# FFN input of a two-block transformer kernel: the activations' high and low parts as one 512-column operand, and new places in SBUF

## The reference

```
h = h + rms_norm(swiglu_ffn(rms_norm(h, norm_ffn_pre[l]), w_ffn_in[l], w_ffn_out[l]), norm_ffn_post[l])
# swiglu_ffn(u, w_in, w_out): z = u @ w_in (1024 x 5632), split in halves of 2816 columns each;
#                             (silu(one half) * (the other half)) @ w_out (2816 x 1024)
```

## Time and profile before

| | |
|---|---|
| median of three runs | 1117.15 us |
| the profiled execution | 1118.65 us |
| its span, first to last instruction | 1117.3 us |
| mean granted TensorE clock | 0.992 |
| FFN input f0, f1 (PE, with the waits in them) | 626.2 to 751.2 us, 924.8 to 1049.8 us |
| FFN output g0, g1 | from 751.2 us, from 1049.8 us |

### The profile page before, as it was taken

The page is one execution under the profiler, slowest core; times in us unless marked ns, Lnnn a source line. Parts: engine busy times, 40 slices in busy tenths (PEclk is TensorE's granted clock), DMA queues, the critical chain, the costliest instruction groups (busy, mean ns, idle before and its releaser), DMA issues.

```text
span 1117.3 us, 19183 instructions
## 1 busy us (share of the span) xinstructions
PE 1091.6 (98%) x7736; PEld 995.6 (89%) x7736; DVE 759.7 (68%) x1416; ACT 592.2 (53%) x1050; POOL 47.2 (4%) x48
## 2 busy tenths in 40 slices
PE   8999999899899999999999999999999999999998
PEld 7998888889699999789987899997889779999986
DVE  3588786997678887776677666674466466666643
ACT  4475583555576666335355744454474367444542
POOL 0260000010000000110000000000000000000000
PEclk9999998999999999999999999999999999999999
DMA  9965942554345554664442475545544134555441
GB/s 361 384 215 223 375 190 78 218 195 152 113 171 189 189 189 170 267 241 158 165 151 91 163 272 189 189 170 174 189 165 156 71 135 162 199 184 184 162 164 38
DMA packets 30764, 208.14 MB, mean 186 GB/s; under 512 B 3538, under 2 KB 4050, under 8 KB 6996
## 3 DMA queue, kind: packets, MB, share of 16 engines
q1 hardware_dynamic: 30676, 206.91, 51.4%
HBM read 205.85 MB, written 1.05 MB: 185 GB/s over the span
## 4 chain that ended last, share of the span: by engine, by line
PE 84%; DVE 11%; ACT 3%; issue 2%; DVEq 0%; ACTq 0%
PE ps L409 45%; PE ps L1730 19%; PE ps L643 3%; DVE wlo L368 3%; PE ps L1508 2%; PE ps L427 2%; DVE tm L582 2%; PE ps L2396 1%; PE ps L2428 1%; PE ps L836 1%; PE ps L1857 1%; ACT whi L360 1%; PE ps L652 1%; PE ps L1362 1%; PE ps L440 1%
## 5 line engine op out<-in xcount | busy, mean ns | idle before, releaser
L368 DVE TENSOR_TENSOR wlo<-raw,whi 128x1024 fp32r<-128x1024 f32 (+2 forms) x328 | 372.7, 1178 | 210.5 <-ACT whi L360 210.1
L360 ACT ACTIVATE whi<-raw 128x1024 fp32r<-128x1024 f32 (+2 forms) x328 | 315.7, 1011 | 156.6 <-PE ps L1730 100.8
L409 PE MATMUL ps<-H_h,whi 128*128 128x256 f32 x1376 | 390.5, 284 | 0.0
L409 PE MATMUL ps<-H_h,wlo 128*128 128x256 f32 x1376 | 385.1, 280 | 0.0
L409 PE MATMUL ps<-H_l,whi 128*128 128x256 f32 x1376 | 384.9, 280 | 0.0
L409 PEld LDWEIGHTS ps<-H_h,whi 128*128 128x128 f32 x1376 | 259.4, 189 | 1.9 <-issue 1.7
L409 PEld LDWEIGHTS ps<-H_l,whi 128*128 128x128 f32 x1376 | 259.6, 189 | 0.7 <-issue 0.5
L409 PEld LDWEIGHTS ps<-H_h,wlo 128*128 128x128 f32 x1376 | 259.9, 189 | 0.0
L1730 PE MATMUL ps<-whi,gl_h 128*128 128x512 f32 x264 | 105.3, 399 | 0.6 <-DVE wlo L368 0.6
L1730 PE MATMUL ps<-whi,gl_l 128*128 128x512 f32 x264 | 104.2, 395 | 0.0
L1730 PE MATMUL ps<-wlo,gl_h 128*128 128x512 f32 x264 | 103.8, 393 | 0.0
(11 more groups left out here) (465 smaller groups left out, 1686.7 us busy)
## 6 DMA issues: line engine op xcount, KB each, us to landing
raw<-f SPq DMA_DIRECT2D x44, 1024.0 KB, 4.8
raw<-win SPq DMA_DIRECT2D x27, 1024.0 KB, 6.8
raw<-ada SPq DMA_DIRECT2D x24, 1024.0 KB, 5.1
raw<-up SPq DMA_DIRECT2D x22, 1024.0 KB, 4.8
raw<-g SPq DMA_DIRECT2D x20, 1024.0 KB, 4.8
raw<-pw SPq DMA_DIRECT2D x12, 1024.0 KB, 4.8
raw<-down SPq DMA_DIRECT2D x10, 1024.0 KB, 5.4
raw<-wa SPq DMA_DIRECT2D x4, 1024.0 KB, 10.2
```

The lines of the kernel that those rows point to most:

```text
L360: act.activation(whi[j % NS][:, a:b], raw_of(key)[:, a:b], ACT.Copy).then_inc(w_hi.hit(key, half), 1)
L368: dve.tensor_tensor(wlo[j % NS][:, a:b], raw_of(key)[:, a:b], whi[j % NS][:, a:b].bitcast(F32), ALU.subtract).then_inc(w_lo.hit(key, half), 1)
L409: ins_ = pe.matmul(bank[:, m * 256:(m + 1) * 256], wt[a][:, kt * w + col + m * 128:kt * w + col + m * 128 + 128], act[b][:, k0 + kt, :], s ...
```

## The change

In the two FFN inputs, high and low part of the activations stand side by side in one tensor (`HF`: per k 256 columns high, then 256 columns low). For each m and k PE now issues two matmuls (`double_pe`): the high weights by all 512 columns into a whole bank, and the low weights by the 256 high columns into its left half. So a unit takes two banks (one for each m), and three pairs of banks take turns; 1/rms gets bank 2. The left half of a bank holds two of the three products, the right half the third, so they have to be added: ACT copies both right halves to `uw` (`low_act`), DVE adds the left halves (`total`), and `scale` multiplies `uw` in SBUF.

The order on ACT and DVE changes with it: ACT does `low_act` behind `next_hi`, then `late_hi`, then SiLU; DVE does `total` behind `next_lo`, then `mul_dve`, then `scale`.

In SBUF, `whi`, `wlo`, `HF`, `gl` and `yc` now all have the remainder 384 by 512 bytes. All other users of `H` get it as a view of the same memory that begins 96 bytes later (remainder 480); its high and low tiles alternate. The rest lies at multiples of 32 bytes.

```diff
-        at = -(-(place[0] - lead[0]) // 128) * 128 + lead[0] if n >= 1024 else place[0]
+        at = place[0] if step == 32 else -(-(place[0] - 384) // step) * step + 384
...
-            lead[0] = 32 * (len(whi) + len(wlo))
-            to.append(sb(f"{name}{i}", [128, 2048], F32R))
-    H = pair("H", 8)
+            to.append(sb(f"{name}{i}", [128, 2048], F32R, 512))
+    Hs = sb("H", [128, 8 * 512 + 32], F32R, 512)
+
+    def halves_of(a):
+        hl = Hs[:, a:a + 4096].rearrange("p (k t) -> p k t", t=512)
+        return hl[:, :, 0:256], hl[:, :, 256:512], hl
+
+    HF = halves_of(0)
+    H = halves_of(24)[0:2]
...
-    gl = pair("gl", NF)
+    gl = pair("gl", NF, 512)
...
+    BANK_PAIRS = (0, 3, 5)
+
+    def double_pe(pe, n, c, ready, hook):
+
+        key, first = (n, c), BANK_PAIRS[c % 3]
+        for i in (first, first + 1):
+            ring, at = (G, i) if i < 3 else (M, i - 3)
+            if ring.free[at]:
+                pe.wait_ge(*ring.free[at])
+            ring.free[at] = u_sum(n, c)
+        where[key] = psum[:, first:first + 2, :]
+        j = SAT[key]
+        hi, lo = whi[j % NS], wlo[j % NS]
+        asked = set()
+        for m, kt in [(m, kt) for kt in range(8) for m in range(2)] if c == 0 else [(m, kt) for m in range(2) for kt in range(8)]:
+            if kt // 4 not in asked:
+                asked.add(kt // 4)
+                pe.wait_ge(*w_lo(key, kt // 4))
+            if c == 0 and m == 0:
+                pe.wait_ge(*ready(kt))
+                hook(kt)
+            a = kt * 256 + m * 128
+            for part in ("lo", "hi") if kt else ("hi", "lo"):
+                if part == "hi":
+                    ins_ = pe.matmul(banks[first + m], hi[:, a:a + 128], HF[2][:, kt, :], start=kt == 0, stop=kt == 7)
+                else:
+                    pe.matmul(banks[first + m][:, 0:256], lo[:, a:a + 128], HF[0][:, kt, :], start=False, stop=False,
+                              skip_group_check=True)
+        ins_.then_inc(unit.hit(*key), 1)
+
     def ffn_pe(pe, n, gen, hook):
         for c in range(NF):
-            gemm_pe(pe, (n, c), H, normed(gen) if c == 0 else held, u_rn(n, c), by_k=c == 0, hook=hook if c == 0 else None)
+            double_pe(pe, n, c, normed(gen), hook)
             if c == 1:
-                rn_pe(pe, gen)
+                rn_pe(pe, gen, True)
+
+    def low_act(act, n, c):
+        act.wait_ge(*unit(n, c))
+        if c >= 3:
+            act.wait_ge(*u_mul(n, c - 3))
+        act.activation(uw[c % 3][:], where[n, c][:, :, 256:512], ACT.Copy).then_inc(u_low.hit(n, c), 1)
...
     def ffn_dve(dve, n, gen):
+        def total(c):
+            dve.wait_ge(*unit(n, c))
+            dve.wait_ge(*u_low(n, c))
+            dve.tensor_tensor(uw[c % 3][:], where[n, c][:, :, 0:256], uw[c % 3][:], ALU.add).then_inc(u_sum.hit(n, c), 1)
+
         def scale(c):
             if c == 0:
                 dve.wait_ge(*rn_set(gen))
-            dve.wait_ge(*unit(n, c))
-            dve.tensor_tensor(uw[c % 3][:], v2(where[n, c][:]), bc2(rn[:]), ALU.mult).then_inc(u_rn.hit(n, c), 1)
+            dve.wait_ge(*u_sum(n, c))
+            dve.tensor_tensor(uw[c % 3][:], uw[c % 3][:], bc2(rn[:]), ALU.mult).then_inc(u_rn.hit(n, c), 1)
```

More of the change, by code:

```diff
@@ L154, in build, with sb @@
 def build(nc, ins, out):
-    place, lead = [-(-nc.sbuf_base // 64) * 64], [0]
-    def sb(name, shape, dt=F32):
+    place = [-(-nc.sbuf_base // 64) * 64]
+    def sb(name, shape, dt=F32, step=32):
         n = 4
@@ L161, in sb, with pair @@
             n *= k
-        at = -(-(place[0] - lead[0]) // 128) * 128 + lead[0] if n >= 1024 else place[0]
+        at = place[0] if step == 32 else -(-(place[0] - 384) // step) * step + 384
         place[0] = at + -(-n // 32) * 32
         return nc.alloc_sbuf_tensor_at(name, shape, dt, offset=at)
-    def pair(name, nch):
-        return sb(name + "_h", [128, nch, 256], F32R), sb(name + "_l", [128, nch, 256], F32R)
+    def pair(name, nch, step=32):
+        return sb(name + "_h", [128, nch, 256], F32R, step), sb(name + "_l", [128, nch, 256], F32R, step)
     par, con = sb("par_sb", [128, NPAR]), sb("con_sb", [128, NCON])
-    sst, epst = sb("sst", [128, 72]), sb("epst", [128, 8])
-    cs, ce = sb("cs", [128, 8]), sb("ce", [128, 8])
     mod, gmod = sb("mod", [128, 48]), sb("gmod", [128, 16])
@@ L251, in build @@
     mh = [sb(f"mh{i}", [128, 384]) for i in range(3)]
-    yc = pair("yc", 8)
+    yc = pair("yc", 8, 512)
     place[0] = block2
@@ L265, in build @@
     tap_f = nc.alloc_sbuf_tensor_at("tap_f", [95, 384], F32R, offset=dft_at + 4 * 768)
-    banks = [nc.alloc_psum_tensor(f"ps{i}", [128, 512], F32) for i in range(8)]
+    psum = nc.alloc_psum_tensor("ps", [128, 8, 512], F32)
+    banks = [psum[:, i, :] for i in range(8)]
     SB, TB, OB = banks[3:5], banks[5:7], banks[7]
@@ L1888, in xtile, with spread_act @@
         return where["xt", gen, k % 4][:, k // 4 * 256:k // 4 * 256 + 256]
-    def spread_act(act, gen, gain):
+    def spread_act(act, gen, gain, to=H):
         for k in range(8):
@@ L1894, in spread_act, with spread_dve @@
                 act.wait_ge(*n_lo(gen, k - 4))
-            act.activation(H[0][:, k, :], xtile(gen, k), ACT.Copy, scale=gain(k)).then_inc(n_hi.hit(gen, k), 1)
-    def spread_dve(dve, gen, gain):
+            act.activation(to[0][:, k, :], xtile(gen, k), ACT.Copy, scale=gain(k)).then_inc(n_hi.hit(gen, k), 1)
+    def spread_dve(dve, gen, gain, to=H):
         for k in range(8):
             dve.wait_ge(*n_hi(gen, k))
-            dve.scalar_tensor_tensor(out=H[1][:, k, :], in0=xtile(gen, k), scalar=gain(k), in1=H[0][:, k, :].bitcast(F32),
+            dve.scalar_tensor_tensor(out=to[1][:, k, :], in0=xtile(gen, k), scalar=gain(k), in1=to[0][:, k, :].bitcast(F32),
                                      op0=ALU.mult, op1=ALU.subtract).then_inc(n_lo.hit(gen, k), 1)
@@ L1908, in xroots_act, with rn_pe @@
             root_act(act, gen, t)
-    def rn_pe(pe, gen):
-        b, old = M.take(rn_set(gen))
+    def rn_pe(pe, gen, apart=False):
+        if apart:
+            b, old, G.free[2] = banks[2], G.free[2], rn_set(gen)
+        else:
+            b, old = M.take(rn_set(gen))
         if old:
@@ L2071, in ffn_dve @@
             if c > 0:
-                scale(c - 1)
+                total(c - 1)
             if c > 1:
                 mul_dve(dve, n, c - 2)
+            if c > 0:
+                scale(c - 1)
             if c > 2:
@@ L2078, in ffn_dve @@
                 tap_parts_dve(dve, (c - 18) // 2)
+        total(NF - 1)
+        mul_dve(dve, n, NF - 2)
         scale(NF - 1)
-        mul_dve(dve, n, NF - 2)
         late_lo(dve, n, NF - 3)
```

19 lines of the change are left out of this document (13 added, 6 removed).

## The result

The changed kernel took 1120.43 us (median of seven runs, 1120.16 to 1122.18), the kernel before beside it 1117.04 us (seven runs, 1113.49 to 1117.26). The ratio is 1.0043, 95% interval 1.0030 to 1.0055: slower by 3.4 us by the medians and by 4.8 us by the ratio, where 1.5 us less had been forecast. The profiled execution took 1122.18 us, with a span of 1120.9 us against 1117.3.

The account below looks back on a forecast made before the run. It took PE's matmul steps as the bound (PE busy 98%, chain 84% on PE). Terms -3.9 - 1.3 + 0.8 + 2.9 = -1.5 us gave a median of 1115.6 us, range 1106 to 1121.5.

Parts of the forecast that it names:

- Step of PE elsewhere: PE outside the FFN input: wide matmuls with `gl` stationary -1.3 us, 64 units with `H` moving +0.8 us.
- equal places collide: Rival: operand reads at the same place hinder each other in each matmul, slow steps become the rule; +7 us, chance 0.08.
- Wide steps in g: 792 wide matmuls of g0, g1 and first `down`: step 0.230 for 0.2317 us, -1.3 us, bounds -2.9 and +2.6.
- The FFN input: PE in f0 and f1: a unit takes 5.554 us against 5.642, -3.9 us over 44 units.
- The circle: Loop of ACT and DVE per FFN-input unit: 5.36 us, fits into 5.554 with 0.19 to spare, cost zero.
- Start of the FFN: First units of the FFN input: `whi` starts 0.65 us later, unit 3 still ready 0.6 us early, no cost.
- The ends: End of each FFN input, ACT and DVE chain: 1.47 us later, twice, +2.9 us, bounds 2.4 and 3.4.
- the circle that does not fit: Rival: in f0 and f1 the ACT and DVE loop grows to 5.8 us and delays PE; +6 us, 1121.7, chance 0.10.
- the excess that goes: Rival: equal places halve float32r matmuls' excess time, in FFN input and wide units; about -14 us, 1103, chance 0.14.
- the places that do nothing: Rival: steps stay 0.2325 and 0.1175, FFN input -1.8 us, nothing in g; +1.9 us, 1119.0, chance 0.13.

Follow-up runs that it names:

- h3: Changed kernel with `H` 32 bytes behind the weights' remainder in place of 96, long ends kept: 1113.18 us, ratio 0.9977.
- e2: Changed kernel with `H` at distance 0 from the weights' remainder in place of 96 bytes, tiles still alternating: 1120.59 us, ratio 1.0030.
- g1: Kernel of e5 with `H` 32 bytes behind the weights' remainder in place of 96: 1107.09 us, ratio 0.9910.
- f2: Changed program in the places of the kernel before (weights 384, 416, 448, 480; `H`, `HF`, `gl`, `yc` 480): 1120.46 us, ratio 1.0024.
- h1: Kernel of g1 with the old FFN input: three narrow matmuls, no copy, no addition: 1108.38 us, ratio 0.9935.
- h2: Kernel of g1 with `HF` also 32 bytes behind the weights' remainder, in place of 0: 1107.63 us, ratio 0.9926.
- e4: Kernel of e1 with the old FFN input (three narrow matmuls, no copy or addition) in the new places: 1124.17 us, ratio 1.0065.
- e1: Changed kernel with the low tiles of `H` behind the high ones, not alternating, still 96 bytes off: 1120.91 us, ratio 1.0037.
- e5: Changed kernel with the second unit of g0 and g1 split before the last SiLU, multiplications and ACT's table load: 1115.24 us, ratio 0.9987.
- g2: Kernel of e5 with `H` and `HF` both 64 bytes behind the weights' remainder: 1109.91 us, ratio 0.9932.

## Why the prediction was wrong

**The step that failed: "Step of PE elsewhere", the 64 other units with `H` moving.** It took "a distance of 96 bytes in all buffers, which stands nearest to the slower unit of 5.66 us: about 0.015 us each", +0.8 us, bounds 0 and +1.3. 60 of the 64 units move `H` (the other four hold it stationary and did not change). They went to 5.76 us, about 0.12 each; in all 6.6 us at most by the steps, and about 5.6 by h3 (its 7.3 less the 1.7 by which its narrow steps, 0.6 ns shorter than before, beat the old ones). The slower unit of before mixes distances, 96 for `whi0` and 64 for `wlo0`; it could not say what 96 alone does. e2 shows that 0, which had stood in the faster unit, is as bad once all weights are alike; g1 and h3 show that 32 removes the whole loss. The same two values, 0 and 96, that are harmless in the staggered order (f2) cost 2% in the alike one. So the bounds, taken from the spread over mixed buffers, did not bound anything. The rival "equal places collide" had the kind right and everything else wrong: it wanted +1 us from `H`, a collision of wide matmuls too, and these became faster.

**Wide steps in g: right in sign, too small.** 0.230 was forecast with a near bound of 0.228, it became 0.2272: -4.1 in place of -1.3 us. The sign was luck: the two units of the earlier trace rows suggested that the buffers nearer to `gl` are faster (0.2308 against 0.2325), but over all eleven units of g1 before, even and odd ones average 0.2323 and 0.2325. And the bounds of 0.228 and 0.235 stand in no row; the means of these units lie between 0.2312 and 0.2334.

**The FFN input: half of what was said, and for another reason.** 5.554 us was forecast, it is 5.595, -2.1 us in place of -3.9; the pair, 0.3497, is inside the range 0.345 to 0.352. f2, h1 and h2 show that next to nothing of it is the operand's: in the old places the pair of matmuls costs what three narrow ones do (5.638 against 5.642 us a unit), and in good places it saves 0.3 to 0.6 us in all. At equal columns the number of matmuls hardly counts, and what lies on top of the columns depends on the places. The operand has a merit only beside bad places (e4 against e1), as it replaces narrow steps of 0.1200 by others.

The rule weighed there, a warm step of N/2.4 + 2.5 ns (Trainium skill, "TensorE: Matmul & The Clock Gate", section "Back-to-back issue gap"), fits neither level: the best narrow steps are 116.7 and the best wide ones 227.2 ns, against 109.2 and 215.8 by the rule. The section calls this the gap of an isolated matmul, and for a stream of loads and matmuls it gives about 131 ns at 512 columns, which is further off still. The 2.5 ns that the rule gives for each matmul saved would have been 1.8 us; h1 against g1 shows 0.3 and against h2 0.6.

**The circle: right.** 5.36 us was worked out, 5.33 measured, and no PE wait inside the 22 units; the cover of 0.19 us became 0.26 mainly because the unit was longer. The copy ran beside `wlo` in 0.58 us. Start of the FFN: right, no wait there.

**The ends: right in mechanism, too small.** +2.9 us forecast with bounds of 2.4 and 3.4, 3.65 measured, outside them: the table load came 3.81 us after PE's last matmul of f1 (1057.19 - 1053.38) where 3.6 was forecast, and at f0 ACT was late by itself (its copy starts at 754.57, 0.3 us behind SiLU's start of the unit before). The faster wide steps have a part in it: PE is through the first unit of g 24 x 5.2 ns = 0.12 us sooner and waits that much longer, twice. The clock's fall, +1.5 us in the profiled execution, stood in no term. e5 shows what the two are worth together, 5.2 us.

**The other rivals,** the circle that does not fit (its time is a slip of the sum: -1.5 + 7.6 = +6.1 us on 1117.15 is 1123.3, not 1121.7), the excess that goes, the places that do nothing: none came. The last was nearest for f0 (5.60 us forecast, 5.595 measured), but g gained where it gave nothing.

Without the failed step the other terms at their measured sizes come to -4.1 - 2.1 + 3.65 + 1.5 = -1.1 us. h3 measures -3.2, but its narrow steps are better than those of before by 1.7 us, where the forecast had them worse by 0.8. With that step as forecast the kernel would stand at -3.2 + 1.7 + 0.8 = -0.7 us, an estimate: the sign as forecast, the size too small to be told from no change. So the failed step turned the sign, and the ends had used up most of the gain.

**What stays open.** Why a narrow float32r step costs 2% more at distances 0 and 96 with all weights alike, and not when they are staggered, no run tells; nor why the step at distance 32 has two levels, so that 32 and 64 can't be ranked by single profiles; nor whether the remainder is to be taken by 128 or by 512 bytes, since all differences tried lie under 128. For the next kernel that is a warning: places are to be measured.

## What to carry to other kernels

Where an engine is busy 98% of the time, moving one of its operands is a change of its own. It acts on every instruction that reads the tensor, also outside the code that is edited: count these first (here 2880 matmuls against 2112 in the edited part). A cost of a new arrangement can't be bounded by the parts of a mixed one; run the pure case. And at the seam of two stages, what is added to the last chain is paid in full, unless the next stage's operand is prepared ahead of it, which here cost four lines.

## What the hardware showed beyond that

- Places in SBUF change the step of a float32r matmul by up to 3%: narrow 0.1167 to 0.1200 us (units of `up` in g1 and in the changed kernel), wide with `gl` stationary 0.2272 to 0.2337. With all weights alike, narrow steps with `H` moving are worst at distances 0 and 96 (0.1200, in all seven kernels that have them) and better at 32 and 64.
- For wide matmuls the order differs. With `H` stationary and 512 columns of the weights moving (192 in the kernel, L1700 and L1738) the step is 0.228 us at distance 0 (e2), 0.233 at 32 (g1), 0.2335 at 64 (g2) and 0.234 at 96 (changed kernel). So the distance that is best there is among the worst for the narrow ones.
- At one distance a narrow step has two levels, 0.1167 and 0.1178 us, in stages of one execution (h1: f0 and `up`).
- Two matmuls of 512 + 256 columns cost nearly what three of 256 do: 5.594 against 5.600 us for a unit (g1, h1), and 5.587 against 5.600 at the same distance (h2, h1); each matmul saved brought 0.4 to 0.8 ns.
- The eight profiled kernels that keep the long ends have 16 waits of PE of 1.9 to 2.2 us at g0 and g1. Behind nine of them the granted clock fell to 1.2 GHz (changed kernel at g0, for 3.4 us), behind the others it did not (the same kernel at g1, h3 at both).
